# Two-layer hybrid trunk with a routed mixture of experts: gathered expert rows added by VectorE, a root moved ahead, a third weight unit split in the norm

## The reference

```python
def trunk(...):
    for layer in range(2):
        h = delta_pool_mixer(x, ...) if layer == 0 else rglru_mixer(x, ...)
        x = layer_norm(ALPHA * x + h, ln_mix_g[layer], ln_mix_b[layer])
        f = moe(x, router_w, router_bias, w_gate[layer], w_up[layer], w_down[layer])
        x = layer_norm(ALPHA * x + f, ln_ffn_g[layer], ln_ffn_b[layer])

def moe(x, ...):            # 16 experts, every token goes to two of them
    scores = sigmoid(x @ router_w)
    combine = ...           # (tokens, 16), two weights per token that sum to 1
    for e in range(16):
        h = silu(x @ w_gate[e]) * (x @ w_up[e])          # 1024 -> 512
        y = y + combine[:, e:e+1] * (h @ w_down[e])      # 512 -> 1024

# in the mixer of layer 0, per head:
o = o * rsqrt(mean(o * o, -1) + RMS_EPS) * norm_w * silu(z)
o_b = einsum('btgc,gcd->btgd', pooled, w_group)          # four groups
y = concatenate([o_a, o_b], -1) @ w_out
```

## Time and profile before

| | |
|---|---|
| median of 3 timed runs | 1436.19 us (1433.83 to 1441.01) |
| the profiled execution, its own time | 1432.69 us |
| its span, first to last instruction | 1431.1 us |
| mean granted TensorE clock | 0.945 of full |
| busy: PE, DVE, ACT, POOL | 90%, 66%, 48%, 17% |
| chain that ended last: PE, DVE, ACT | 83%, 10%, 2% |

### The profile page before, as it was taken

One profiled execution on the slowest core, in us unless ns is written; L12 is line 12 of the kernel. 1 busy time (PEld: TensorE's weight loads), 2 busy tenths in 40 slices (PEclk: granted clock), 3 DMA queues, 4 the chain that ended last, 5 costly groups with the idle time before them and its releaser, 6 DMA issues.

```text
span 1431.1 us, 16721 instructions
## 1 busy us (share of the span) xinstructions
PE 1292.7 (90%) x6609; PEld 1025.7 (72%) x6609; DVE 944.4 (66%) x1261; ACT 693.5 (48%) x808; POOL 240.7 (17%) x256
## 2 busy tenths in 40 slices
PE   7999978887898599999999889799976999999995
PEld 7989867774345488888886488786445888888861
DVE  4874355441355689899994665643656999999936
ACT  4433222221023378888883333570233888888821
POOL 4431352211200100000003200351001000000032
PEclk9999979997998699999999989999977999999998
DMA  5421040001533399999996311122155999999841
GB/s 169 143 67 60 19 134 1 1 14 38 173 136 140 126 398 417 413 412 417 419 380 206 122 32 59 59 108 74 74 216 188 405 411 414 413 415 417 345 132 66
DMA packets 76111, 294.50 MB, mean 206 GB/s; under 512 B 8176, under 2 KB 34505, under 8 KB 51200
## 3 DMA queue, kind: packets, MB, share of 16 engines
q1 hardware_dynamic: 64704, 252.51, 45.9%
q0 software_dynamic: 7296, 26.22, 5.1%
q10 hardware_dynamic: 4032, 14.68, 2.5%
HBM read 266.50 MB, written 26.89 MB: 205 GB/s over the span
## 4 chain that ended last, share of the span: by engine, by line
PE 83%; DVE 10%; issue 2%; ACT 2%; DMA 1%; POOL 1%; SPq 0%; DVEq 0%; ACTq 0%; POOLq 0%
PE bank L1085 12%; PE bank L1087 12%; PE bank L1086 12%; PE bank L1014 6%; PE bank L1177 5%; PE bank L649 4%; PE bank L650 4%; PE bank L1001 4%; PE bank L694 3%; PE bank L695 3%; PE bank L1079 2%; PE bank L1025 1%; PE bank L770 1%; PE bank L1114 1%; PE bank L638 1%
## 5 line engine op out<-in xcount | busy, mean ns | idle before, releaser
L1961 DVE TENSOR_TENSOR UNIT_LOW<-work,UNIT_HIGH 128x2048 fp32r<-128x2048 f32 x192 | 436.5, 2290 | 49.0 <-ACT UNIT_HIGH L1258 48.7
L1258 ACT ACTIVATE UNIT_HIGH<-work 128x2048 fp32r<-128x2048 f32 x192 | 365.9, 1919 | 82.4 <-PE bank L1087 82.2
L1085 PE MATMUL bank<-UNIT_HIGH,XGT_HIGH 128*128 128x512 f32 x512 | 204.4, 399 | 5.0 <-DVE XGT_LOW L2130 5.0
L1087 PE MATMUL bank<-UNIT_HIGH,XGT_LOW 128*128 128x512 f32 x512 | 201.1, 393 | 0.0
L1086 PE MATMUL bank<-UNIT_LOW,XGT_HIGH 128*128 128x512 f32 x512 | 200.6, 392 | 0.0
L2499 POOL DMA_INDIRECT work<-x_rows,idx_all x32 | 38.9, 1214 | 615.9 <-PE bank L1079 416.1
L1258 ACT ACTIVATE work<-bank 128x512 f32<-128x512 f32 (+3 forms) x178 | 74.6, 474 | 109.6 <-PE bank L763 30.4
L1085 PEld LDWEIGHTS bank<-UNIT_HIGH,XGT_HIGH 128*128 128x128 f32 x512 | 97.2, 190 | 25.0 <-DVE XGT_LOW L2130 5.8
L1087 PEld LDWEIGHTS bank<-UNIT_HIGH,XGT_LOW 128*128 128x128 f32 x512 | 96.9, 189 | 21.0
L1086 PEld LDWEIGHTS bank<-UNIT_LOW,XGT_HIGH 128*128 128x128 f32 x512 | 97.2, 190 | 19.5
L1085 PE MATMUL bank<-UNIT_HIGH,HT_HIGH 128*128 128x512 f32 x256 | 101.0, 395 | 4.7 <-issue 4.7
(11 more groups left out here) (487 smaller groups left out, 2605.5 us busy)
## 6 DMA issues: line engine op xcount, KB each, us to landing
work<-in_moe_w_gate_dram SPq DMA_DIRECT2D x64, 1024.0 KB, 7.5
work<-in_moe_w_up_dram SPq DMA_DIRECT2D x64, 1024.0 KB, 7.8
work<-in_moe_w_down_dram SPq DMA_DIRECT2D x64, 1024.0 KB, 7.9
y_rows<-work ACTq DMA_DIRECT2D x28, 512.0 KB, 8.1
work<-in_ab_w_in_dram SPq DMA_DIRECT2D x10, 1024.0 KB, 5.5
work<-in_c_w_in_dram SPq DMA_DIRECT2D x8, 1024.0 KB, 5.4
x_rows<-X SPq DMA_DIRECT2D x8, 512.0 KB, 2.6
X<-in_x_prompt_dram SPq DMA_DIRECT2D x4, 512.0 KB, 5.0
```

What stands on the lines that cost most here:

```text
L1085: mm(to, x[0], high, start=start, stop=False)
L1087: return mm(to, x[1], high, start=False, stop=stop)
L1258: return nc.scalar.activation(out, in_, ACT.Copy, scale=scale)
L1961: V.tensor_tensor(UNIT_LOW[home(l, n)][:, :], work[:, UNIT * home(l, n):UNIT * home(l, n) + UNIT], UNIT_HIGH[n % HIGHS][:, :].bitcast(F32) ...
```

## The change

Four edits go together.

1. UNIT_HIGH's homes are put in another order so that the third slot does not lie over XT. The third unit of a layer is then rounded by ACT and split by DVE in the norm ahead of the routing, beside the last tile's transposes, and no longer ahead of the first gather. `places_of_late` follows the index at once, and the fourth and fifth unit's splits come behind it, the latter behind the first `x_low`.
2. In the sample step ACT takes the root ahead of the wait for "ut" and of the group copies.
3. In the combination the diagonal products go. ACT multiplies X by ALPHA in experts 5 to 9, one tile each. DVE adds the gathered rows to X, weight by weight, in ten operations of 1024 columns after its last operation of expert 15, each waiting for the one before it; `stats` then uses the factor 1. PE keeps the two products of the late experts. The output of expert 14 is copied out of PSUM by ACT ahead of LATE_COLS instead of behind them.
4. The semaphore `hist1_in` is merged into `hist_in`.

```diff
         UNIT_HIGH = [placed(f"UNIT_HIGH{s}", at, off, (UNIT,)) for s, (at, off) in enumerate(
-            ((WORK_AT, 28672), (WORK_AT, 32768), (XT_AT, 0), (XT_AT, 2048), (WORK_AT, 30720)))]
-        EARLY_SPLITS = 2
+            ((WORK_AT, 28672), (WORK_AT, 32768), (WORK_AT, 30720), (XT_AT, 0), (XT_AT, 2048)))]
+        EARLY_SPLITS = 3
...
             def combine(l):
                 q = 2 * l + 1
-                pe.wait_ge(y_out_sb, NE * l + LATE[0] + 1)
-                pe.wait_ge(late_made, 11 * (l + 1))
-                for t, ys in enumerate(y_homes(l)):
-                    r = ROWS[t]
+                pe.wait_ge(late_act, (NT + 1) * (l + 1))
+                for t in range(NT):
                     if t >= 2:
                         pe.wait_ge(norm_sum, q * NT + t - 1)
-                    pe.wait_ge(ysel_in[t], 32 * (l + 1))
-                    parts = [(WEIGHT_DIAG[k][t][0:r, 0:r], ys[k][0:r, :]) for k in range(2)] + \
-                            [(LATE_COLS[:, j, tile_cols(t)], YO[e % 2]) for j, e in enumerate(LATE)]
-                    for n, (w, y) in enumerate(parts):
-                        if n == 3:
-                            pe.wait_ge(y_out_sb, NE * (l + 1))
+                    for j, e in enumerate(LATE):
+                        pe.wait_ge(y_out_sb, NE * l + e + 1)
                         for half in range(2):
-                            last = mm(bank[2 * (t % 2) + half][0:r, :], w, y[:, 512 * half:512 * half + 512],
-                                      start=(n == 0), stop=(n == 3))
+                            last = mm(bank[2 * (t % 2) + half][0:ROWS[t], :], LATE_COLS[:, j, tile_cols(t)],
+                                      YO[e % 2][:, 512 * half:512 * half + 512], start=(j == 0), stop=(j == 1))
...
   ACT, sample step
                 e_act.end(copy(OWN_W, heads_of(6, P, n).rearrange("p h (s l) -> p h s l", s=NS), -1.0), 0, "nw")
+                act.wait_ge(rms_eps, 1)
+                nc.scalar.activation(gB[0:NH, 0, 0:TP], gB[0:NH, 0, 0:TP], ACT.Sqrt).then_inc(rms_root, 1)
                 e_pe.wait(act, 0, "ut")
...
-                act.wait_ge(rms_eps, 1)
-                nc.scalar.activation(gB[0:NH, 0, 0:TP], gB[0:NH, 0, 0:TP], ACT.Sqrt).then_inc(rms_root, 1)
...
   ACT, norm ahead of the routing
-                    to_channels(q + 1, (3, 4))
+                    to_channels(q + 1, (3,))
+                    round_unit(q // 2, 2)
+                    to_channels(q + 1, (4,))
...
   ACT, experts
+                    if 5 <= e < 5 + NT:
+                        act.wait_ge(xrows_out, 16 * NT * (l + 1))
+                        x = X[0:ROWS[e - 5], e - 5, :]
+                        copy(x, x, ALPHA).then_inc(late_act, 1)
                 h_high(NE - 1)
+                result(LATE[0])
                 act.wait_ge(late_ps, l + 1)
...
-                for e in LATE:
-                    result(e)
+                result(LATE[1])
...
   DVE, stats
-                        last = V.scalar_tensor_tensor(x[:, c], x[:, c], ALPHA, bank[2 * (t % 2) + half][0:r, :],
-                                                      ALU.mult, ALU.add)
+                        last = V.scalar_tensor_tensor(x[:, c], x[:, c], 1.0 if q % 2 else ALPHA,
+                                                      bank[2 * (t % 2) + half][0:r, :], ALU.mult, ALU.add)
...
   DVE, norm ahead of the routing, route, experts
                     to_channels(q + 1, (4,))
+                    split_unit(l, 2)
...
-                split_unit(l, EARLY_SPLITS)
                 dve.wait_ge(idx_ps, l + 1)
                 V.tensor_copy(idx_all[:, 0, :], bank[3][:, 0:NE]).then_inc(idx_ready, 1)
...
-                for n in range(EARLY_SPLITS + 1, HIGHS):
+                places_of_late(l)
+                split_unit(l, EARLY_SPLITS)
+                x_low(0)
+                for n in range(EARLY_SPLITS + 1, HIGHS + 1):
                     split_unit(l, n)
-                x_low(0)
-                places_of_late(l)
-                split_unit(l, HIGHS)
...
                 h_low(NE - 1)
-                dve.wait_ge(late_ps, l + 1)
-                for k in range(2):
-                    for t in range(NT):
-                        last = V.tensor_scalar(WEIGHT_DIAG[k][t], ident[:, :], wsel[:, k, t:t + 1], None, ALU.mult)
-                last.then_inc(late_made, 1)
                 overflow(l)
+                dve.wait_ge(late_act, (NT + 1) * l + NT)
+                for t, ys in enumerate(y_homes(l)):
+                    dve.wait_ge(ysel_in[t], 32 * (l + 1))
+                    for k in range(2):
+                        x = X[0:ROWS[t], t, :]
+                        mine(V.scalar_tensor_tensor(x, ys[k][0:ROWS[t], :], wsel[0:ROWS[t], k, t:t + 1], x, ALU.mult, ALU.add))
+                        mine.settle()
```

More of the change, by code:

```diff
@@ L304, in hybrid_trunk @@
                      [xt_flat[:, 4096 + P * t:4224 + P * t] for t in range(NT - 1)] + [lnp_free[:, 1792:1920]]]
-        WEIGHT_DIAG = LATE_ROWS
         def y_homes(l):
@@ L333, in hybrid_trunk @@
         router_in, lists_zeroed = sem("router_in"), sem("lists_zeroed")
-        ss_in, wg_in, wo_in, wri_in, hist1_in = sem("ss_in"), sem("wg_in"), sem("wo_in"), sem("wri_in"), sem("hist1_in")
+        ss_in, wg_in, wo_in, wri_in = sem("ss_in"), sem("wg_in"), sem("wo_in"), sem("wri_in")
         wo_early_in = sem("wo_early_in")
@@ L383, in hybrid_trunk @@
         h_ps, ht_high, ht_low, y_out_sb = sem("h_ps"), sem("ht_high"), sem("ht_low"), sem("y_out_sb")
-        late_made, late_ps = sem("late_made"), sem("late_ps")
+        late_made, late_ps, late_act = sem("late_made"), sem("late_ps"), sem("late_act")
         operands = ["x0", "x1", "x2", "w0", "w1", "x3", "x4"] + [f"w{c}" for c in range(2, 16)]
@@ L506, in mixer1 @@
                 sp.wait_ge(ysel_in[3], 32)
-                sp.dma_start(lhist_rows[0:24, :], state_lru_conv[0].rearrange("s j c -> (s j) c")).then_inc(hist1_in, 16)
-                sp.dma_start(lstate_rows[0:NS, :], state_lru[0]).then_inc(hist1_in, 16)
-                sp.dma_start(par_rows1[0:32, :], c_conv_w[0].rearrange("j (c p) -> (j c) p", p=P)).then_inc(hist1_in, 16)
+                sp.dma_start(lhist_rows[0:24, :], state_lru_conv[0].rearrange("s j c -> (s j) c")).then_inc(hist_in, 16)
+                sp.dma_start(lstate_rows[0:NS, :], state_lru[0]).then_inc(hist_in, 16)
+                sp.dma_start(par_rows1[0:32, :], c_conv_w[0].rearrange("j (c p) -> (j c) p", p=P)).then_inc(hist_in, 16)
                 for n, src in enumerate((c_conv_b, c_b_r, c_b_i, c_lambda)):
                     sp.dma_start(par_rows1[32 + 8 * n:40 + 8 * n, :], src[0].rearrange("(c p) -> c p", p=P))\
-                      .then_inc(hist1_in, 16)
+                      .then_inc(hist_in, 16)
                 win = c_w_in[0].rearrange("(k p) c -> p k c", p=P)
@@ L1151, in late_transposed @@
             def late_transposed(l):
-                pe.wait_ge(late_made, 11 * l + 10)
+                pe.wait_ge(late_made, 2 * NT * (l + 1))
                 for j in range(2):
@@ L1213, in mixer1 @@
             def mixer1():
-                pe.wait_ge(hist1_in, 16 * 7)
+                pe.wait_ge(hist_in, 16 * (5 + 7))
                 pe.wait_ge(norm_sum, 2 * NT - 1)
@@ L1452, in norm @@
                             act.wait_ge(lru_h, KD)
-                        if t < EARLY_SPLITS:
+                        if t < 2:
                             round_unit(q // 2, t)
@@ L1534, in experts @@
                     copy(LATE_COLS[:, j, 0:TP], bank[2 + j][:, :])
-                copy(LATE_COLS[:, :, TP:T], bank[7][:, 0:2 * TS].rearrange("p (j c) -> p j c", j=2))
-                for e in LATE:
-                    result(e)
+                copy(LATE_COLS[:, :, TP:T], bank[7][:, 0:2 * TS].rearrange("p (j c) -> p j c", j=2)).then_inc(late_act, 1)
+                result(LATE[1])
                 overflow(l)
@@ L2013, in norm @@
                         finish(t)
-                        if 1 <= t <= EARLY_SPLITS:
+                        if 1 <= t <= 2:
                             split_unit(l, t - 1)
```

## The result

The changed kernel took 1386.31 us (median of 4 runs, 1384.98 to 1391.89) against 1438.6 us before (4 runs, 1433.83 to 1441.17): ratio 0.9657, 95% interval 0.9629 to 0.9684 (the two medians alone would give 0.9637, inside that interval). The forecast was 1389. The profiled execution took 1386.39 us with a span of 1384.8, so 46.3 us less than the profiled one before; the sum of the prediction was 46.2. On a second chip the same kernel took 1390.98 us against 1434.45: ratio 0.9697 (0.9684 to 0.9711). The two ratios put the gain at 49 and 43 us, their intervals at 41 to 53; more can't be said of the size.

The account below looks back on a forecast made before the run. PE was taken to carry most of the chain, with gains at three seams where it waits or does other work. 9.4 + 5.8 + 31.0 = 46.2 us off 1432.69 gave 1386.5, stated as 1389; own range 1382 to 1394, 8-in-10 range 1380 to 1404.

Parts of the forecast that it names:

- Sample step: 9.4 us forecast: Sample step: moving the root closes PE's gap for 6.8 us, and PE's full clock adds 2.6; ends 6.8 and 9.8.
- the 2.6 us put down to the clock: Sample step: without the gap L896 and the first L905 run at PE's full clock, saving 2.6 us.
- Head: 2.9 a layer: Head of the experts: index 1.1 us earlier, first gather's descriptor work 1.8 us shorter; 2.9 us a layer, 5.8 in all.
- Updates: 1.33 us each: Combination: each 1024-column update on DVE takes 1.29 us plus 0.04 for the wait on the one before; ten take 13.3.
- Stats to stats: 15.1 us: Norm behind the combination: DVE takes 3.0 + 3.3 + 4.4 + 4.4 = 15.1 us from first to last stats.
- Combination: 15.5 a layer: Combination: DVE's updates replace PE's diagonals, so the last stats starts 15.5 us earlier a layer, 31.0 in all.
- signs that it is wrong: Listed signs of failure: DVE still waits for PE in the norm, updates wait for gathers, or ACT's expert roundings stand further apart.
- Rival 2: Combination: PE's clock falls to half and PE bounds again; 27 us more than forecast, 1416; chance 0.07.
- Rival 1: Combination: gathers and updates hold each other up, updates 0.39 us longer, 7.8 us in both layers, 1397; chance 0.13.
- The earlier copy of expert 14's output: End of the experts: copied ahead of LATE_COLS, it may let PE's last products start some 1.7 us earlier.
- ALPHA copies: Experts 5 to 9: five copies ALPHA * X cost ACT at most 1.2 us each and fit in its idle time.
- rival 4: Experts: the seams close but the time comes back there, since loads and not PE set the pace; 1431; chance 0.02.

Follow-up runs that it names:

- the filled gap: Kernel before plus six 128 x 512 products on PE ahead of its wait for "un" in the sample step: 1437.48 us, ratio 1.0025.
- alone: Changed kernel with edits 1 and 2 taken back, so only the combination edit and the merged semaphore: 1404.97 us, ratio 0.9789.
- changed kernel's second profile: Changed kernel run again, unchanged, on the second chip: 1390.98 us (5 runs).
- the first attempt: Changed kernel with the last tile's gathered rows added by PE diagonals and DVE adding tiles 2 and 3's bias in norms behind the experts: 1386.34 us, ratio 0.9664.
- the attempts: The first attempt, and the changed kernel with its diagonals, DVE's bias in the last norm only, and a reordered sample step: 1382.52 us, ratio 0.9636.

## Why the prediction was right

- **Sample step: 9.4 us forecast.** The first trace gives 9.7 between the anchors (10.3 by the output projection's start, which has 0.6 from ahead of it). Over all profiled runs, four with the code of before (48.74, 50.17, 50.47, 53.25) and seven with the root moved (39.02 to 42.41, mean 41.08), it is 50.66 - 41.08 = 9.6 us. The size was right and one reason incomplete: the 2.6 us put down to the clock were shared between clock and POOL's chain, as the filled gap showed. L896 and the first L905 did run at full clock in all seven, but in six of them the clock fell at the next wait, which the prediction left out. And the term is a distribution: a single profile is off its mean by up to 2.6 us before and 2.1 after. Both traces that the forecast is held against are the fastest of their code in this stage, and these two errors cancel: that is luck.
- **Head: 2.9 a layer.** Measured 2.9 and 2.8 in the first trace. The index came 1.2 us earlier (1.1 forecast) and the gather's descriptor work saved 1.79 (1.8 forecast). What failed is the attribution to edit 1 as a whole: the third unit's split in the norm was not needed.
- **Updates: 1.33 us each.** Measured 1.285, and 1.32 from one to the next. The start behind h_low was 0.25 us behind its end in layer 1, as forecast, and 0.52 in layer 0.
- **Stats to stats: 15.1 us.** Measured 15.48 (0.53 of it the wait for PE at half clock) and 14.86.
- **Combination: 15.5 a layer.** Measured 14.9 twice in the first trace, 15.5 and 15.8 alone, 15.5 and 14.1 in the changed kernel's second profile. The difference is the two small waits, for PE and for a gathered tile. The prediction had named both as signs that it is wrong; they came, and were small. Rival 2 (half clock) came true for one tile and cost 0.5 us, where its price was 27. Rival 1 had a price of 7.8 us for longer updates, and these did not come: in layer 0 the first three, with gathers beside them, and the next five take 1.285 us each.
- **The wait for a gathered tile** is not explained by the updates that hold POOL. The eighth gather of layer 1 is held for about 0.95 us in the first trace (1.89 us long for 0.94), but just as long in four runs in which DVE did not wait. What differs is the landing: 8.6 us behind the gather's start in the first trace, 8.8 in the second and 8.7 in the first attempt, where it was held for 0.2 us only and DVE waited 1.89; 6.9 to 7.4 in those four. Without the hold it would have landed in the first trace at about the moment it was wanted, so there hold and late landing came together. Why it landed late was not traced.
- **The earlier copy of expert 14's output** was named as one reason for PE being ready, 1.7 us earlier; it gave 3.4. Taken back it changed nothing: PE's first two sums then end some 13.5 and 17.0 us behind h_low, and the stats that need them start at 14.4 and 17.4.
- **ALPHA copies** cost nothing, as forecast; **time given back in the experts** (rival 4) did not occur: 280.06 us for 280.05 in layer 0, 281.18 for 280.42 in layer 1.

Forecast were 9.4 + 5.8 + 31.0 = 46.2 us, measured between the anchors 9.7 + 5.7 + 29.8 = 45.2. The other 1.1 of the 46.3 us between the two spans lie in stretches that the change does not touch: the agreement to 0.1 us is luck. By stage it is 1 us, in two traces that are both fast in the sample step.

## What to carry to other kernels

When an engine's wait goes, follow every other chain that started at the released operation: here a helper's product was due 0.85 us later and would have taken the place of the wait, had it not been covered too. Compare stages between their own anchors and not whole spans: with unchanged code this stage took 48.7 to 53.3 us, a spread of 4.5 us beside the 5.7 that the edit at the head was worth. Replacing a matrix product by vector updates paid here because DVE was idle for 14.5 us a layer; afterwards the balance could be shifted back by one tile of five.

## What the runs showed of the hardware

- An indirect DMA's descriptor work on POOL waits for the end of the DVE operation with two SBUF inputs that runs when it starts, then takes 0.75 to 0.95 us, and goes on beside the next such operation. It does not wait for a pause, and one that starts just ahead of the operation is not held: 0.93 us in layer 0, begun at 753.97 where the first update begins at 754.05. On POOL, layer 1 of the changed kernel, where the first update ends at 1340.89 and the second at 1342.22:

```profile
1339.82 1.89 POOL L2476 DMA_INDIRECT work<-y_rows,pos_i  x1 [0.30 <-issue]
1342.01 0.98 POOL L2476 DMA_INDIRECT work<-y_rows,pos_i  x1 [0.30 <-issue]
```

  The first is held 0.95 us. A gather beside a string of updates lost at most one of them. The Trainium skill (SBUF — State Buffer, SBUF: two separate sides) says that DVE with two SBUF inputs and GpSimd exclude each other for a whole instruction, and from that the prediction had up to four updates for the last issues; in these traces the updates, too, did not get longer.
- The reverse is dearer: POOL's addition of 2.35 us held DVE's one-column L1989 for 2.33 us and the gain of the last tile for 3.32 in the last norm, which is where the attempts found 1.9 us. DVE and POOL, end of the changed kernel:

```profile
1373.11 2.33 DVE L1989 SCALAR_TENSOR_TENSOR lnw<-lnw 64x1 f32<-64x1 f32 x1
...
1376.75 3.32 DVE L1996 TENSOR_TENSOR X<-X,LNP 64x1024 f32<-64x1024 f32 x1 [0.17 <-ACT X L1436]
```

```profile
1373.09 2.34 POOL L2495 TENSOR_TENSOR X<-X,LNP 128x1024 f32<-128x1024 f32 x1 [1.97 <-DVE X L1996]
1376.65 2.34 POOL L2495 TENSOR_TENSOR X<-X,LNP 128x1024 f32<-128x1024 f32 x1 [1.23 <-DVE X L1996]
```

- Behind one and the same wait of 2.70 us PE's clock fell to 1.2 GHz in one profile of the changed kernel (0.54 of full in 355.8 to 357.8) and stayed at 2.4 GHz in the other (1.00 in 354 to 358). Twelve filler instructions in the longest gap kept it up in the gap, but it was at half behind the next two waits, of 1.64 and 0.85 us.
